# An eight-group recurrence on one core: right sides, outputs and product rounds laid between the levels of the next group

## The reference

```python
def rwkv7_scan(r, decay, k, v, kk, a, s0, reverse):
    def step(S, inp):
        r_t, w_t, k_t, v_t, kk_t, a_t = inp
        sa = jnp.einsum('bhvk,bhk->bhv', S, -kk_t)
        S = (S * w_t[:, :, None, :] + sa[..., None] * (kk_t * a_t)[:, :, None, :]
             + v_t[..., None] * k_t[:, :, None, :])
        return S, jnp.einsum('bhvk,bhk->bhv', S, r_t)
```

## Time and profile before

| | before |
|---|---|
| median of 3 runs | 2581.63 us (2581.1 to 2583.8) |
| the profiled execution | 2581.12 us, span 2579.3 us |
| PE busy, share of the span | 2251.7 us, 87% |
| DVE busy | 969.1 us, 38% |
| ACT busy | 744.3 us, 29% |
| POOL busy | 931.8 us, 36% |
| mean granted TensorE clock | 0.927 |

### The profile page before, as it was taken

How to read it: one execution, slowest core, us unless ns; L and a number is a source line. 1 busy time by engine, 2 the same in 40 slices (tenths; PEclk the granted TensorE clock), 3 DMA queues, 4 the chain that set the end, 5 groups by cost and what they waited for, 6 DMA issues and landing times.

```text
span 2579.3 us, 35529 instructions
## 1 busy us (share of the span) xinstructions
PE 2251.7 (87%) x15423; PEld 1832.2 (71%) x15423; DVE 969.1 (38%) x1412; ACT 744.3 (29%) x1081; POOL 931.8 (36%) x421
## 2 busy tenths in 40 slices
PE   5999999799938778787899999799999797468996
PEld 2778778587417677675677877577888596468996
DVE  3321221522695544545622122532132501635212
ACT  2422222533031211113522222522222444125343
POOL 0334434442060110103434434344444353016884
PEclk9999999899969987898999999899999898658998
DMA  9463363220000000003364353264232140023551
GB/s 330 158 204 123 96 231 122 82 90 13 0 0 2 2 2 2 2 4 130 99 198 151 98 188 131 94 196 166 98 98 82 41 142 28 0 71 117 190 178 66
DMA packets 176091, 259.66 MB, mean 101 GB/s; under 512 B 3925, under 2 KB 146275, under 8 KB 175876
## 3 DMA queue, kind: packets, MB, share of 16 engines
q1 hardware_dynamic: 173194, 252.39, 29.2%
q10 hardware_dynamic: 2746, 5.04, 0.5%
HBM read 256.37 MB, written 1.05 MB: 100 GB/s over the span
## 4 chain that ended last, share of the span: by engine, by line
PE 77%; DVE 14%; ACT 4%; issue 2%; DMA 1%; ACTq 0%; SPq 0%; POOL 0%; DVEq 0%; POOLq 0%
PE psum L957 77%; DVE arena L1833 2%; ACT arena L668 1%; ACT u_hi L673 1%; DVE arena L1807 1%; DVE arena L1857 1%; DVE h L1617 1%; DMA arena<-in_ada_w 1%; DVE arena L1774 1%; DVE arena L1855 1%; DVE arena L1785 1%; DMA arena<-in_x 0%; DVE tmp L1630 0%; ACT tmp L718 0%; ACTq L581 0%
## 5 line engine op out<-in xcount | busy, mean ns | idle before, releaser
L2047 POOL TENSOR_TENSOR w_lo<-arena,w_hi 128x1024 fp32r<-128x1024 f32 x332 | 812.2, 2452 | 1130.0 <-ACT w_hi L640 1127.6
L957 PE MATMUL psum<-u_hi,w_hi 128*128 128x512 f32 (+1 forms) x1888 | 698.7, 370 | 74.0 <-ACT u_hi L673 38.8
L957 PE MATMUL psum<-u_hi,w_lo 128*128 128x512 f32 (+1 forms) x1888 | 688.0, 365 | 0.0
L957 PE MATMUL psum<-u_lo,w_hi 128*128 128x512 f32 (+1 forms) x1888 | 668.6, 362 | 0.0
L640 ACT ACTIVATE w_hi<-arena 128x1024 fp32r<-128x1024 f32 x332 | 348.4, 1055 | 743.9 <-PE psum L957 730.8
L957 PE MATMUL psum<-arena 64*64 64x64 f32 (+7 forms) x5828 | 438.1, 276 | 98.6 <-DVEq L1813 27.7
L957 PEld LDWEIGHTS psum<-u_hi,w_hi 128*128 128x128 f32 x1888 | 361.9, 192 | 171.4 <-issue 41.1
L957 PEld LDWEIGHTS psum<-arena 64*64 64x64 f32 (+4 forms) x5828 | 358.8, 166 | 170.4 <-issue 63.3
L957 PEld LDWEIGHTS psum<-u_hi,w_lo 128*128 128x128 f32 x1888 | 362.3, 192 | 54.3
L957 PEld LDWEIGHTS psum<-u_lo,w_hi 128*128 128x128 f32 x1888 | 357.5, 190 | 52.9 <-issue 0.2
L1587 DVE TENSOR_TENSOR tmp<-psum,tmp 128x512 f32<-128x512 f32 (+1 forms) x88 | 54.9, 624 | 593.6 <-ACT tmp L692 593.6
(11 more groups left out here) (246 smaller groups left out, 1630.6 us busy)
## 6 DMA issues: line engine op xcount, KB each, us to landing
arena<-in_ada_w SPq DMA_DIRECT2D x48, 1536.0 KB, 7.0
arena<-in_ffn_wg SPq DMA_DIRECT2D x44, 1024.0 KB, 5.5
arena<-in_ffn_wu SPq DMA_DIRECT2D x44, 1024.0 KB, 8.1
arena<-in_ffn_wd SPq DMA_DIRECT2D x20, 2048.0 KB, 8.1
arena<-in_ev_w_in SPq DMA_DIRECT2D x6, 2048.0 KB, 7.9
arena<-in_od_w_in SPq DMA_DIRECT2D x6, 2048.0 KB, 8.3
arena<-in_ffn_wd SPq DMA_DIRECT2D x4, 1024.0 KB, 5.0
arena<-in_ev_w_out SPq DMA_DIRECT2D x2, 2048.0 KB, 10.7
```

The source lines that it names most:

```text
L957: return pe.matmul(dst, w, x, start=first_, stop=last, skip_group_check=True)
L2047: pool.tensor_tensor(piece_shape(split_lo(pc), src), src, piece_shape(split_hi(pc).bitcast(F32), src), ALU.subtract).then_inc(S("lo_done"), 1)
```

## The change

It keeps all values and changes the order and the split of the recurrence's work.

- The four matrices no longer come at once. `strict` multiplies only A's operands, and it does so for the next group in level 6 of the current one; `turn_strict` turns it behind that level. The other matrices come in three rounds (`rest`), each of eight 128-column or four 256-column products, in levels 3, 4 and 5, between the Z products and the factors. DVE's `take_rest` copies a round ahead of that level's factors.
- The right side stays behind level 6. Solution and outputs of a group now run in level 1 of the next one (`solve` ahead of the factors, `outputs` behind them); tu and ar exist twice for that.
- ar has no halves of zeros any more: products with the state use 64 rows. The sign of kk moves into the preparation, the state's two scalings per chunk become one (`carry`), and the last chunk has no state update.
- `by_parts` uses only the blocks that change at levels 5 (32x32) and 6 (64x64).
- Slots of chunks 1 to 3 are made by POOL, in two steps; those of chunk 0 on DVE in another order. ACT's exponentials are spread over levels 1 to 4 of even groups; the turned keys move to levels 5 and 6.
- The gate products move from the preparation to levels 5 and 6 of the last group, their weights from ACT's DMA queue to SP's.

The core of the diff (removed lines of the loops stand in the kernel above):

```diff
-        gate, kk = arena[:, 43008:45056], arena[:, 16384:18432]
-
-        ar = arena[:, 0:4096].rearrange("p (d c e a t) -> p d c e a t", d=2, c=CT, e=2, a=2)
+        gate, kk = arena[:, 22528:24576], arena[:, 16384:18432]
+        ar = arena[:, 0:4096].rearrange("p (b d c a t) -> p b d c a t", b=2, d=2, c=CT, a=2)
         bk = arena[:, 18432:20480].rearrange("p (d c a t) -> p d c a t", d=2, c=CT, a=2)
         bkt = arena[:, 4096:6144].rearrange("p (d a c) -> p d a c", d=2, a=2)
         nm = arena[:, 6144:10240].rearrange("p (d h a t) -> p d h a t", d=2, h=4, a=4)
-        tu = arena[:, 10240:12288].rearrange("p (d a h t) -> p d a h t", d=2, a=2, h=4)
+        nm_of = arena[:, 6144:10240].rearrange("p (d c e a t) -> p d c e a t", d=2, c=2, e=2, a=4)
+        tus = [at.rearrange("p (d a h t) -> p d a h t", d=2, a=2, h=4)
+               for at in (arena[:, 10240:12288], arena[:, 43008:45056])]
...
+                    sp.wait_ge(S("slots_b"), 12)
+                    sp.dma_start(g_up_late, A["rw_g_up"][0]).then_inc(S("ld_lora"), 16)
...
+                for gi in range(8):
+                    j, hf = gi // 2, gi % 2
+                    for lv in range(1, LEVELS):
+                        m = 1 << lv
                         for d in range(2):
-                            act.wait_ge(S("x_mm"), 2 * gi + d + 1)
+                            act.wait_ge(S("z_mm"), 2 * (LEVELS * gi + lv) + d + 1)
+                            act.activation(blocks(zs[:, d].rearrange("p h t -> p (h t)"), m, d),
+                                           blocks(bank[d], m, d), ACT.Copy).then_inc(S("zs"), 1)
+                        if hf == 0 and j < 3 and lv < 5:
+                            decays_of(j + 1, (lv - 1) // 2, (lv - 1) % 2 * 2, 2 if lv % 2 else 5)
+                        if hf == 0 and lv >= 5:
...
+                def by_parts(lv, dst, w, x, k, r, n):
+                    m = 1 << lv
+                    for at in range(0, P, max(64, 2 * m)):
+                        if m < 32:
+                            ks = rs_ = ns = slice(at, at + 64)
+                        else:
+                            ks, rs_, ns = (slice(at + m * i, at + m * i + m) for i in (k, r, n))
+                        ins = mm(dst[rs_, ns], w[ks, rs_], x[ks, ns], True, True)
+                    return ins
...
+                def rest(gi, r):
+                    j, hf = gi // 2, gi % 2
+                    if r:
+                        pe.wait_ge(S("r_done"), 6 * gi + 2 * r)
+                    elif gi:
+                        pe.wait_ge(S("o_add"), 2 * gi)
+                    if gi == 0:
+                        pe.wait_ge(S("slots_a"), 2)
+                        pe.wait_ge(S("first_slots"), 6)
+                    elif hf == 0:
+                        pe.wait_ge(S("slots_b"), 4 * j)
+                    for cc in range(2):
+                        c = 2 * hf + cc
+                        if r:
+                            d = r - 1
+                            for e, hp in enumerate(half_rows):
+                                ins = mm(bank[6 + e][:, cc * 2 * P:(cc + 1) * 2 * P], bk[hp, d, c, 1],
+                                         ar[hp, j % 2, d, c].rearrange("p a t -> p (a t)"), True, True)
+                        else:
+                            for d in range(2):
+                                for e, hp in enumerate(half_rows):
+                                    ins = mm(bank[6 + e][:, (2 * d + cc) * P:(2 * d + cc + 1) * P], bk[hp, d, c, 0],
+                                             ar[hp, j % 2, d, c, 1], True, True)
+                    ins.then_inc(S("r_mm"), 1)
...
+                    for d in range(2):
+                        for cc in range(2):
+                            c = 2 * hf + cc
+                            dst = [bank[6 + e][:, (2 * d + cc) * 64:(2 * d + cc + 1) * 64] for e in range(2)]
+                            for e, hp in enumerate(half_rows):
+                                mm(dst[e], ar[hp, j % 2, d, c, 0], state[hp, d, c], True, False)
+                            for e in range(2):
+                                hh = 2 * cc + e
+                                ins = mm(dst[e], nm[:, d, hh, 2], vt[:, chunk_of(d, j), vcol(gi, hh)], False, True)
+                    ins.then_inc(S("x_mm"), 1)
...
+                strict(0)
+                turn_strict(0)
+                for gi in range(8):
+                    j, hf, tu = gi // 2, gi % 2, tus[gi % 2]
+                    for lv in range(1, LEVELS):
                         for d in range(2):
...
+                            pe.wait_ge(S("tu"), 2 * (2 * (gi * LEVELS + lv - 1) + d + 1))
+                            for hh in range(4):
+                                ins = by_parts(lv, bank[d][:, hh * P:(hh + 1) * P], nm[:, d, hh, 0], tu[:, d, 0, hh],
+                                               d, 1 - d, d)
+                            ins.then_inc(S("z_mm"), 1)
+                        if lv == 1 and gi:
+                            solve(gi - 1)
+                        if lv in (3, 4, 5):
+                            rest(gi, lv - 3)
+                        if lv == LEVELS - 1 and gi < 7:
+                            strict(gi + 1)
+                        if lv == LEVELS - 1 and hf == 0:
+                            turn_keys(j, 1)
+                        if lv == LEVELS - 1 and gi == 7:
+                            gates(2)
+                        for d in range(2):
+                            pe.wait_ge(S("zs"), 2 * (gi * (LEVELS - 1) + lv - 1) + d + 1)
+                            if lv < LEVELS - 1:
                                 for hh in range(4):
...
+                                    by_parts(lv, bank[2 + d][:, hh * P:(hh + 1) * P], tu[:, d, 1, hh], zs[:, d, hh],
+                                             1 - d, 1 - d, d)
                             for hh in range(4):
...
+                                ins = by_parts(lv, bank[4 + d][:, hh * P:(hh + 1) * P], zs[:, d, hh], tu[:, d, 1, hh],
+                                               1 - d, d, 1 - d)
+                            ins.then_inc(S("d_mm"), 1)
+                        if lv == 1 and gi:
+                            outputs(gi - 1)
+                        if lv == 5 and hf == 0:
+                            turn_keys(j, 0)
+                        if lv == 5 and gi == 7:
+                            gates(0)
+                    if gi < 7:
+                        turn_strict(gi + 1)
+                    right_side(gi)
+                solve(7)
+                outputs(7)
...
+                def take_rest(gi, r):
+                    ve.wait_ge(S("r_mm"), 3 * gi + r + 1)
+                    for e in range(2):
+                        src = bank[6 + e].rearrange("p (c a t) -> p c a t", c=2, a=2)
+                        if r:
+                            mk = mask_of[:, r - 1].unsqueeze(1).to_broadcast([P, 2, 2, P])
+                            ve.copy_predicated(nm_of[:, r - 1, :, e, 2:4], mk, src).then_inc(S("r_done"), 1)
+                        else:
+                            mk = mask_of[:, :, 1].unsqueeze(2).to_broadcast([P, 2, 2, P])
+                            ve.copy_predicated(nm_of[:, :, :, e, 1], mk, src).then_inc(S("r_done"), 1)
...
+                take_strict(0)
+                double(0, 0)
+                for gi in range(8):
+                    for lv in range(1, LEVELS):
+                        if lv == 1 and gi:
+                            take_solution(gi - 1)
+                        if lv == LEVELS - 1 and gi < 7:
+                            take_strict(gi + 1)
+                        if lv in (3, 4, 5):
+                            take_rest(gi, lv - 3)
+                        double(gi, lv)
+                        if lv == 1 and gi:
+                            take_outputs(gi - 1)
+                    if gi < 7:
+                        double(gi + 1, 0)
+                take_solution(7)
+                take_outputs(7)
...
+                for gi in range(7):
+                    j, hf = gi // 2, gi % 2
+                    if gi:
+                        pool.wait_ge(S("sa_mm"), 2 * gi)
+                    reset(gi + 1)
+                    if j < 3 and hf == 0:
                         for d in range(2):
-                            pool.wait_ge(S("exped"), 2 * j + d + 1)
+                            pool.wait_ge(S("exped"), 2 * (j + 1) + d + 1)
                             if j:
                                 pool.wait_ge(S("os_mm"), 4 * j)
...
+                            for a, src in enumerate((kk, zr)):
+                                pool.tensor_tensor(ar[:, (j + 1) % 2, d, :, a], part(src, d, j + 1), decays[d][a], ALU.mult)\
+                                    .then_inc(S("slots_a"), 1)
+                    elif j < 3:
+                        for q, src in enumerate((aa, kd)):
+                            pool.wait_ge(S("r_mm"), 3 * gi + (3 if q else 1))
```

(52 more changed lines are left out.)

418 lines of the change are left out of this document (170 added, 248 removed).

## The result

The changed kernel takes 2512.6 us (2502.9 to 2514.4, 4 runs), the kernel before 2581.4 us beside it: ratio 0.973, interval 0.972 to 0.975. Forecast were 2470 us and at most 2504. So 69 us were won where 111 were expected.

What follows compares the result with a forecast made beforehand. No engine was full, so waits bound the recurrence. With group 0's early start, seven periods of 34.0 us, gates and end, it ends at 1050.4 instead of 1161.3, saving 110.9 us: 2470 us, range 2446 to 2504.

Steps and rivals of the forecast that it cites:

- every duration at the upper clock: Steady group of the recurrence: all durations counted at the upper clock, granted clock 1.0 from the second group on.
- Clean period 34.0: One steady group of the recurrence: 14.0 + 9.0 + 10.0 + 0.2 + 0.8 = 34.0 us.
- Start: Before group 0's rounds: level 0 copies at 773.5 instead of 780.86 us, round 0 ending at 785.3.
- End: After T(8) = 1044.1: xs, solution, outputs and additions take 6.3 us, ending at 1050.4 instead of 1161.3.
- the levels with a round: Levels 3 to 5: a level goes from 3.40 to 4.5 us because PE and DVE meet.
- DVE's slots leave the path: Chunks 1 to 3: eight products move to POOL, 5.7 us in each of six groups, covered; POOL at some 50 us.
- keys, gates, the moved weights and ACT's exponentials: Turned keys 0.2 us a group on average, gates +1 in group 7, gate weights' queue 0, exponentials covered.
- DVE slowed by POOL: Rival: masked copies beside POOL's products get slower, 4.5 us lost in six groups, 27 in all: 2497; chance 0.07.
- PE full: Rival: DVE's waits fall away through narrow blocks at levels 5 and 6, period nears 30.5 us: 2446; chance 0.11.
- Moved tail: Rival: in-order PE waits at solution or outputs, some 5 us a group return, 35 in all: 2505; chance 0.07.
- Drains: Rival: changes between 64x64 and wider tiles cost 2.7 instead of 0.8 us: 2483, or 2494; 0.22 with other small waits.
- Slower: Rival: clock stays at 1.2 GHz through the stretch because PE keeps stopping for DVE: 2691 us; chance 0.02.

Runs made afterwards that it cites:

- fillers: Changed kernel plus one unread identity product behind the factors of levels 3, 4 (256 columns) and 5 (512 in odd groups): 2492.9 us.
- statefull: Changed kernel with the state products of right side and outputs reading all 128 rows instead of 64, mixing two heads, for time alone: 2488.0 us.
- before_narrow: Kernel before, with only the narrow tiles of levels 5 and 6 put in: 2620.9 us, ratio 1.016.
- fill_long: Changed kernel with unread products at levels 3, 4 and 5, all of 512 columns in every group: 2519.6 us.
- filler5: Changed kernel with an unread product only at level 5 (512 columns in odd groups, 256 in even ones): 2503.5 us.

## Why the prediction was wrong, point by point

The stretch should have ended at 1050.4 and ended at 1095.2: 44.8 us. They are, by the prediction's own steps:

- **Clock, "every duration at the upper clock": 25.7 us.** Seven steps averaged 39.37, against 35.70 with fillers (six of 35.8 to 35.9 and the last of 34.7), (39.37 - 35.70) x 7. This is the step that failed. I had made the low clock a rival with 0.02, all or nothing, and let only holes in PE's work bring it. It comes and stays with PE busy 4.00 of 4.00, behind level 5, for some 3 to 20 us at a time, in six of seven steps; in odd groups it follows a wait of 1.23 us, where I expected none above 0.9. The prediction's own signs of being wrong, a period over 38 and a clock at 0.5 past 790, both came. A hint stood in the trace of before: the chain's piece of 128 records behind level 6 took 9.30 us in seven groups and 14.15 in group 4.

```profile
1001.82 14.15 PE psum L957 x128
```

- **Clean period 34.0 where 35.70 was right: 11.9 us.** The outputs were copied from the earlier trace rows although the change gives their state products another shape: 1.2 (`statefull`). Eight right-side products with half the rows were taken at 1.3 and cost 1.8: 0.5. The bound 0.9 to 1.8 was right, the middle wrong. Together 1.7, all of the difference.
- **Start: 4.0 us.** Round 0's copies began at 789.34 where 785.3 was forecast. I let two of DVE's first products run beside POOL; but POOL's queue goes on with the resets of the next tu, so that all four did, and level 1 still ran at 1.2 GHz.

```profile
764.43 1.80 DVE L1886 TENSOR_TENSOR arena<-arena 128x512 f32<-128x512 f32 x1 [0.15 <-DVE arena L1877]
...
767.29 2.94 POOL L2199 COPY arena<-ident 128x1024 f32<-128x1024 f32 x2
...
769.26 1.52 DVE L1887 TENSOR_TENSOR arena<-arena 128x512 f32<-128x512 f32 x1
```

- **End: 3.2 us.** From the last first round (1064.91) to the last addition 30.3 instead of 27.1; the clock is 0.50 from 1088 to 1092 us, in solution and outputs.

Right were: the levels with a round (4.4 to 4.6 for 4.5); that rounds aren't free but cheaper inside; that DVE's slots leave the path (POOL 42 us instead of 34); that keys, gates, the moved weights and ACT's exponentials cost nothing that can be seen.

Of the rivals, *DVE slowed by POOL* falls: in group 0 a round's copies (793.96, 1.35 us for two) ran beside POOL's product of the slots and took what they take alone.

```profile
794.06 2.50 POOL L2221 TENSOR_TENSOR arena<-arena,tmp 128x512 f32<-128x512 f32 x2 [5.24 <-ACT tmp L805]
```

*PE full* falls: waits of 0.2 to 1.2 us stay. *Moved tail* falls: solution and outputs stand without a wait in one piece of PE. *Drains* held in part: some 0.5 to 0.9 us a group hang on the outputs' changes of shape. *Slower* named the low clock but had its cause only in part (three of the falls, those in even groups, have no such stop of PE just ahead) and its form wrong: the clock falls for parts of groups. `before_narrow` shows what such falls cost without the pipeline that pays for them.

What a rule would have said: by the Trainium skill, TensorE: Matmul & The Clock Gate, Part 1, the clock follows how busy PE has recently been. The rows from 1040 to 1048 us, a fall out of a PE busy 4.00 of 4.00, don't agree, if busy is what the profile counts; `fill_long` doesn't either. Whether the chip counts otherwise than the profile isn't shown.

## What to carry to other kernels

Where work is laid between other work, price both engines' queues: that part of the sum came within 3%. Multiply a full-clock sum only after looking for single groups in the old trace in which the same records took half as long again; if there is one, the low clock needs a price for a part of the groups and not a chance for all. And a smaller tile is not a cheaper one by its size: 32x32 and 64x64 pieces at two levels saved some 2 us a group and, without fillers, cost as much in clock.

## What was not expected of the hardware

- The clock can fall while PE is busy without a hole (1040 to 1048 us) and stays low so (916 to 932 us: 4.00 of 4.00, 0.50); in `filler5` each fall cost 4.5 us of a 36 us group.
- Narrow tiles at two of seven levels slowed the kernel before by 42 us.
- Three products a group that nobody reads, laid in waits, made the kernel 20 us faster; with all of them at 512 columns it was 7 us slower than with none. Which amount is right was found by trying; nothing here gives the rule.
- A 64-row weight costs what a 128-row one does when 64 columns pass (0.22 us).
